# FFN of a two-layer streaming trunk: TensorE's steps written out, additions moved ahead of convolution taps; chunk scan with 128-column products, fewer TensorE instructions and a new order

## The reference

```python
def conv_ffn(h, buf, w_up, conv_w, conv_b, w_down):          # D_FF = 3072
    u, new_buf = causal_dwconv(h @ w_up, buf, conv_w, conv_b)  # 3 taps along time
    g, val = jnp.split(u, 2, axis=-1)
    return (jax.nn.gelu(g) * val) @ w_down, new_buf

def step(s, inp):                                             # RWKV-7, per head (16 heads of 64)
    r_t, w_t, k_t, v_t, aa_t, bb_t = inp
    sa = jnp.einsum('bhij,bhj->bhi', s, aa_t)
    s = s * w_t[:, :, None, :] + sa[..., None] * bb_t[:, :, None, :] + v_t[..., None] * k_t[:, :, None, :]
    return s, jnp.einsum('bhij,bhj->bhi', s, r_t)
...
for layer in range(DEPTH):
    hn = rmsnorm(x, norm_mix[layer])
    ...                                                       # y: RG-LRU mixer or RWKV-7 mixer
    x = x + y
    y, fb = conv_ffn(rmsnorm(x, norm_ffn[layer]), ...)
    x = x + y
```

## Time and profile before

| | us |
|---|---|
| median of 3 runs (lowest, highest) | 3423.7 (3421.11, 3430.75) |
| the profiled execution | 3425.41 |
| its span, first to last instruction | 3423.6 |
| PE busy | 3074.2 (90%) |
| DVE, ACT, POOL busy | 1705.8, 1156.4, 964.8 |

### The profile page before, as it was taken

How to read it: one execution, slowest core, us unless ns; L and a number is a source line. 1 busy time by engine, 2 the same in 40 slices (tenths; PEclk the granted TensorE clock), 3 DMA queues, 4 the chain that set the end, 5 groups by cost and what they waited for, 6 DMA issues and landing times.

```text
span 3423.6 us, 73739 instructions
## 1 busy us (share of the span) xinstructions
PE 3074.2 (90%) x32214; PEld 2966.1 (87%) x32214; DVE 1705.8 (50%) x1691; ACT 1156.4 (34%) x1334; POOL 964.8 (28%) x521
## 2 busy tenths in 40 slices
PE   5999699999999997699968888887899999999996
PEld 5888699999999997699957777776799999999996
DVE  6555654544454546102116776772464454444455
ACT  4634322211222214433326666664222221111222
POOL 2222232222222223213313334333222222222221
PEclk9999899999999998799979999998999999999998
DMA  2111011111111110332222122212111111111111
GB/s 97 42 41 39 25 38 44 44 43 43 43 43 43 43 44 19 137 128 83 89 88 61 52 66 67 67 33 88 38 38 44 38 44 44 44 38 38 44 44 64
DMA packets 87544, 185.80 MB, mean 54 GB/s; under 512 B 28896, under 2 KB 51936, under 8 KB 87264
## 3 DMA queue, kind: packets, MB, share of 16 engines
q1 hardware_dynamic: 80352, 154.73, 14.3%
q10 hardware_dynamic: 6912, 26.84, 1.9%
HBM read 145.01 MB, written 36.53 MB: 53 GB/s over the span
## 4 chain that ended last, share of the span: by engine, by line
PE 62%; issue 13%; DVE 12%; POOL 6%; ACT 5%; DMA 1%; SPq 0%; ACTq 0%; DVEq 0%; POOLq 0%
PE PS L1105 51%; PE PS L1270 10%; POOL WL L897 4%; DVE T L1545 3%; ACT T L461 2%; DVE T L1535 1%; POOL PL L897 1%; DVE X L1535 1%; DVE G L1535 1%; DVE HL L1535 1%; PE PS L1223 1%; POOL HL L897 1%; ACT L461 1%; DVE M L1550 1%; DVE NN L1535 1%
## 5 line engine op out<-in xcount | busy, mean ns | idle before, releaser
L897 POOL TENSOR_TENSOR WL<-RAW,WH 128x1024 fp32r<-128x1024 f32 x204 | 497.6, 2439 | 1586.3 <-ACT WH L461 1582.6
L1105 PE MATMUL PS<-HH,WH 128*128 128x364 f32 x3456 | 778.6, 334 | 91.1 <-POOL HL L897 42.8
L1105 PE MATMUL PS<-HH,WL 128*128 128x364 f32 x3456 | 774.4, 333 | 0.0
L1105 PE MATMUL PS<-HL,WH 128*128 128x364 f32 x3456 | 772.2, 332 | 0.0
L1105 PEld LDWEIGHTS PS<-HH,WH 128*128 128x128 f32 x3456 | 608.2, 191 | 104.0 <-issue 61.3
L1105 PEld LDWEIGHTS PS<-HH,WL 128*128 128x128 f32 x3456 | 612.6, 191 | 0.0
L1105 PEld LDWEIGHTS PS<-HL,WH 128*128 128x128 f32 x3456 | 610.4, 191 | 0.0
L1545 DVE SCALAR_TENSOR_TENSOR T<-T,FP 128x1092 f32<-128x1092 f32 x192 | 456.4, 2377 | 6.8
L1535 DVE TENSOR_TENSOR X<-PS,X 128x1092 f32<-128x1092 f32 x224 | 290.3, 1296 | 272.8 <-PE PS L1105 268.4
L461 ACT ACTIVATE WH<-RAW 128x1024 fp32r<-128x1024 f32 x204 | 216.6, 1062 | 408.8 <-PE PS L1105 388.3
L1550 DVE COPY T<-FP 128x2 f32<-128x2 f32 x96 | 16.3, 170 | 675.2 <-ACT T L461 675.2
(11 more groups left out here) (156 smaller groups left out, 3438.6 us busy)
## 6 DMA issues: line engine op xcount, KB each, us to landing
RAW<-weights SPq DMA_DIRECT2D x204, 512.0 KB, 3.4
scratch<-T ACTq DMA_DIRECT2D x32, 546.0 KB, 2.8
scratch<-SR ACTq DMA_DIRECT2D x16, 546.0 KB, 2.8
X<-xT SPq DMA_DIRECT2D x8, 546.0 KB, 7.7
yT<-T SPq DMA_DIRECT2D x8, 546.0 KB, 2.8
T<-scratch_m SPq DMA_DIRECT2D x8, 512.0 KB, 4.6
LW<-scratch SPq DMA_DIRECT2D x16, 192.0 KB, 2.7
KK<-scratch SPq DMA_DIRECT2D x16, 192.0 KB, 3.3
```

The costliest lines, as they stand in the source:

```text
L897: pool.tensor_tensor(out, full, hi, ALU.subtract).then_inc(*t.made(event))
L1105: mm = pe.matmul(acc[:, j, :], a, b[:, j * CW:(j + 1) * CW], start=(i == 0 and q == 0), stop=(i == len(blocks) - 1 and q == 2))
```

## The change

In the FFN, PE's loop over turns is gone and its steps are written out; the other engines keep their loops. DVE's `take(0)` goes ahead of tap 1, `take(1)` ahead of tap 0, and `take(2)` ahead of the product of gate and value. At the first FFN's end ACT's two `sh_hi` stand among the first four squares. In the scan, `solved` and the W half of `moves_and_left` make one 128-column product where there were two of 64 columns; `products` and `key_turn` load both halves of [b, k] of head 0 as 128 columns at once, three matmuls a chunk where there were four; SP waits for each of the five loads before it issues the next; and the order within the interval is new on PE, ACT, DVE and POOL.

```diff
 # SP, loads of job + 4
-                        sp.wait_ge(*t.at("k_g", 8 * (job + 2)))
+                        sp.wait_ge(*t.at("k_g", 6 * (job + 2)))
                         sp.wait_ge(*t.at("k_bonus", job + 2))
                     for tile, j in ((LW, 0), (KK, 4), (AA, 1), (RR, 3), (VV, 5)):
                         load(b, f, tile, j, f"dma_in{b}")
+                        if job >= -1:
+                            sp.wait_ge(*t.at(f"dma_in{b}", t.n[f"dma_in{b}"]))
...
 # ACT, norm behind the first FFN
-            for q in range(2):
-                act.wait_ge(*t.next("mu_w"))
-                run(TR[:, 6 + q, 0:D], T[:, q, 0:D], ACT.Copy, "sh_hi")
-            norm(m, added(m - KT), n, "two")
+            plus = added(m - KT)
+            def added_and_shift(k):
+                if k in (1, 3):
+                    act.wait_ge(*t.next("mu_w"))
+                    run(TR[:, 6 + k // 2, 0:D], T[:, k // 2, 0:D], ACT.Copy, "sh_hi")
+                plus(k)
+            norm(m, added_and_shift, n, "two")
...
 # PE, FFN
-                with pe.Fori(0, FFN_TURNS) as turn:
-                    t.enter(turn, FFN_TURN)
-                    a, b = m, n
-                    for s in (1, 2):
-                        a, b = step(a, b)
-                        a, b = down(a, b, s - 1)
-                    t.leave(FFN_TURNS)
-                m, n = m + 24 * FFN_TURNS, n + 12 * FFN_TURNS
+                for s in range(1, STEPS - 1):
+                    m, n = step(m, n)
+                    m, n = down(m, n, s - 1)
...
 # PE, scan
-                            mul(tile(3 + s, h, i - a), MT[HALF[1 - h], i, :], RA[HALF[1 - h], s, i - a, :],
-                                ("k_wv" if s else "k_w") if i == z - 1 else None)
+                            mul(PAIR[HALF[h], (i - a) * P:(i - a + 1) * P], MT[HALF[1 - h], i, :],
+                                RA[HALF[1 - h], i - a, :, :].rearrange("p s c -> p (s c)"), "k_w" if i == z - 1 else None)
...
+                            for h in range(HEADS):
+                                mul(PAIR[HALF[h], i * P:(i + 1) * P], W[HALF[h], i, :], G[HALF[h], a + i, h, CHUNK:],
+                                    "k_rp" if a + i == z - 1 else None)
...
+                        mul(PS[:, 3, (i - pa) * CHUNK:(i - pa + 1) * CHUNK], BK[HALF[0], i, :, :].rearrange("p s c -> p (s c)"),
+                            IST[HALF[0], :], end)
                         for s in range(2):
-                            for h in range(HEADS):
-                                mul(tile(3 + h, (h + s) % 2, i - pa), BK[HALF[h], i, s, :], IST[HALF[h], :],
-                                    "k_tb" if i == pz - 1 else None)
+                            mul(tile(4, 1 - s, i - pa), BK[HALF[1], i, s, :], IST[HALF[1], :], end)
...
 # DVE, conv: additions ahead of taps
                 for j in range(last - 1, -1, -1):
-                    if j == 0 and between is not None:
-                        take(between, 0)
                     back = last - j
+                    if between is not None:
+                        take(between + back - 1, back - 1)
...
 # DVE, order of an interval (first part)
                 near()
                 scan()
+                one_more()
                 key()
-                one_more()
+                grown(1)
                 centred()
                 weighted()
-                grown(1)
-                removal()
-                reading()
                 mask(2)
                 transfer()
+                reading()
                 grown(2)
+                removal()
```

More of the change, by code:

```diff
@@ L736, in bank, with pair @@
                     return PS[half, n, 0:chunks_ * CHUNK].rearrange("p (n c) -> p n c", c=CHUNK)
+                def pair(n, s, half=slice(0, P)):
+                    return PAIR[half, 0:n * P].rearrange("p (n s c) -> p n s c", s=2, c=CHUNK)[:, :, s, :]
                 def turned(k):
@@ L758, in spread_out @@
                         act.wait_ge(*t.next("k_ra", 4))
-                        run(RA[:, :, 0:z - a, :].rearrange("p s n c -> p s (n c)"), PS[:, 3:5, 0:(z - a) * CHUNK], ACT.Copy, "k_rae")
+                        run(RA[:, 0:z - a, :, :].rearrange("p n s c -> p s n c"),
+                            PS[:, 3:5, 0:(z - a) * CHUNK].rearrange("p s (n c) -> p s n c", c=CHUNK), ACT.Copy, "k_rae")
                 def norm_ln():
@@ L774, in solved_values @@
                     if has_s:
-                        act.wait_ge(*t.at("k_wv", 2 * job + 2))
+                        act.wait_ge(*t.at("k_w", 2 * job + 2))
                         for h in range(HEADS):
-                            run(UV[HALF[h], a:z, h, :], bank(4, z - a, HALF[h]), ACT.Copy, "k_sae")
+                            run(UV[HALF[h], a:z, h, :], pair(z - a, 1, HALF[h]), ACT.Copy, "k_sae")
                 def solved_keys():
@@ L782, in solved_keys @@
                         act.wait_ge(*t.at("k_w", 2 * job + 2))
-                        run(W[:, 0:z - a, :], bank(3, z - a), ACT.Copy, "k_we")
+                        run(W[:, 0:z - a, :], pair(z - a, 0), ACT.Copy, "k_we")
                 def decay_in():
@@ L1442, in products @@
                     for i in range(ga, gz):
+                        end = "k_g" if i == gz - 1 else None
+                        ar = [AR[HALF[h], i, :, :].rearrange("p s c -> p (s c)") for h in range(HEADS)]
+                        mul(PS[:, 3, (i - ga) * P:(i - ga + 1) * P], BK[HALF[0], i, :, :].rearrange("p s c -> p (s c)"), ar[0], end)
                         for s in range(2):
[L1444 to L1446 removed]
+                            mul(tile(4, 1 - s, i - ga, P), BK[HALF[1], i, s, :], ar[1], end)
                 def value_turn():
@@ L1483, in interval @@
                 means()
-                solved(0)
-                solved(1)
+                solved()
                 seed()
+                moves_and_left(2)
                 fresh_state()
-                moves_and_left(2)
+                grow(2)
+                variances()
                 fresh_out()
-                variances()
+                link(0)
+                left_times(3)
+                key_squares()
                 value_turn()
-                grow(2)
-                link(0)
-                key_squares()
-                left_times(3)
-                products(0)
                 link(1)
                 grow(3)
-                products(1)
+                link(2)
+                products(0)
+                link(3)
                 bonus_sums()
                 left_times(4)
-                link(2)
+                products(1)
+                grow(4)
                 key_turn()
-                link(3)
-                grow(4)
                 link(4)
-                lower(0)
                 left_times(5)
                 link(5)
+                lower(0)
                 lower(1)
@@ L1722, in step @@
                         if s and j:
-                            take(m + 1, 1)
+                            take(m + 2, 2)
                         dve.wait_ge(*t.next("gelu"))
@@ L1735, in ffn @@
                         a = step(s, a)
-                        take_all(a, False, first=2)
+                        take_all(a, False, first=3)
                         a += KT
@@ L1740, in ffn @@
                 m = step(STEPS - 1, m)
-                take_all(m, False, first=2)
+                take_all(m, False, first=3)
                 m += KT
@@ L1873, in masked @@
                         ga, gz = groups(pb, 4)[g]
[L1874 removed]
+                        dve.wait_ge(*t.next("k_g", 3))
                         n = gz - ga
@@ L1883, in transfer @@
                         dve.wait_ge(*t.at("k_rp", 2 * job + 2))
-                        tt(PT[:, 0:z - a, :], bank(4, z - a), wide(IST[:, :], z - a), ALU.add, "k_pp")
+                        tt(PT[:, 0:z - a, :], pair(z - a, 1), wide(IST[:, :], z - a), ALU.add, "k_pp")
                 def reading():
```

59 lines of the change are left out of this document (27 added, 32 removed).

## The result

The changed kernel takes 3517.5 us (median of 4 runs, 3504.8 to 3528.4), the kernel before beside it 3425.0 us (3421.1 to 3430.8): a ratio of 1.027, 95% interval 1.023 to 1.031. The prediction was 3333 us, range 3298 to 3368, faster with 0.95. It is slower by 92 us. The profiled execution took 3504.8 us, the fastest of the four, with a mean granted clock of 0.943 against 0.936 to 0.940 in the others.

The account below looks back on a forecast made before the run. PE was taken to bound the FFNs, and PE's work plus its waits the scan. Terms 33.2 + 25.6 + 7.4 + 9 + 5 + 10 = 90.2 us off 3425.4 gave 3335.2, predicted as 3333 us at the median, range 3298 to 3368.

Parts of the forecast that it names:

- Additions ahead of taps: Both FFNs: DVE's earlier additions end PE's 1.51 us wait in each of 22 steps; gain 33.2 us.
- ACT at the end of the first FFN: End of first FFN: squares start earlier, PE's 5.54 us wait and half the lower-clock time go; gain 7.4 us.
- PE's steps written out: Second FFN: four turn edges of PE's loop go, 6.39 us each; gain 25.6 us.
- Rivals 3: Second FFN: the turn-edge wait stays, as a delayed fetch met in straight code too; 3359 us, chance 0.05.
- 4: FFN steps: additions held up beside POOL, so the step's wait moves; 3345 us, chance 0.05.
- rival 5: Scan: SP's single loads come late and ACT waits for the keys, making the kernel slower; 3477 us, chance 0.03.
- Scan, 128-column products: Scan: gains in `solved` and `moves_and_left` outweigh losses in `products` and `key_turn`; gain 9 us, bounds +17 and -26.
- `products` then lose 0.10 us: Scan, six chunks and two recorded passes: a 128-column load makes `products` 115 ns a chunk and pass, from 107.
- `key_turn` ... +0.65 us: Scan, six chunks and two recorded passes: `key_turn` goes from 61 to 115 ns a chunk and pass.
- 53 ns for one stream of 128 columns in a row half: Scan: a 128-column stream fits under a pair's 59 ns load, so `solved` halves its pairs, -0.70 us for six chunks.
- fewer instructions: Scan: 816 matmuls fewer mean 13 instruction fetches fewer; gain 5 us, bounds 0 and 25.
- order and loads: Scan: half of the 13.1 us waits for B go, -6, and single loads no longer crowd DMA engines, -4; gain 10 us.

Follow-up runs that it names:

- experiment 3: Kernel before plus 13 patterns of float32 matmuls behind the second FFN, each timed alone; the mixed patterns took 0.78 (`products`) and 0.62 us (`key_turn`) a chunk.
- Experiment 6: Changed kernel with `products` and `key_turn` grouped by shape: all chunks' 128-column instructions first, then all 64-column ones; 3398.2 us, ratio 0.994.
- experiment 12: Kernel before plus seven further matmul patterns behind the second FFN, only the patterns timed; three that alternate shapes took rounds of 0.64, 0.54 and 0.64 us.
- experiment 4: Kernel before with only the FFNs' part: PE's steps written out, additions ahead of taps, ACT's two shift casts moved; 3360.6 us, ratio 0.981.
- 1: Also written experiment 1: changed kernel with `products` and `key_turn` as before, four 64-column instructions a chunk; 3337.9 us, ratio 0.976.
- experiment 8: Experiment 1 without the 128-column outputs: `solved` and `moves_and_left` with 64 moving columns, as before; 3361.5 us, ratio 0.983.
- 10: Experiment 1 without the wait on SP that lets the loads go one by one; 3338.3 us, ratio 0.976.
- Experiment 5: Changed kernel with `products` and `key_turn` as one 128-column instruction for each half, two a chunk in place of three; 3335.0 us, ratio 0.975.
- Experiment 2: Kernel before with only the changed kernel's new `products` and `key_turn`; 3545.9 us, ratio 1.037.

## Why the prediction was wrong

The FFNs' terms held. *Additions ahead of taps* and *ACT at the end of the first FFN* (16.6 + 7.4 = 24.0 us to the first norm): 23.5 in the profile. Second FFN (16.6 + 25.6 = 42.2): 43.6. *PE's steps written out* (25.6) gave 24.4 in its own stage. Rivals 3 and 4 did not come, nor did rival 5.

The steps that failed are in *Scan, 128-column products*.

- **"`products` then lose 0.10 us", "`key_turn` ... +0.65 us".** These terms were the cost of a wider load, with everything else overlapping as before. They measured 96 and 84 us in all, 4.2 and 3.7 us an interval. In parts, by an estimate from experiment 3: the wide stationary on one half has no partner beside it, 61 us; two changes of shape a chunk and function, 136 x (337 + 279 ns) = 84 us; the remaining 35 us I put down to the lower clock. Experiment 6 met the first part only with its own changes left out (22 us), so each part is good to some 20 us. The last is a remainder and not shown on its own: the clock fell behind such stretches in the scan and in the patterns (0.86 in the changed scan, 0.90 with `key_turn` alone new, 0.98 grouped). I had priced instructions by shape and never asked what two shapes next to each other do. The bound of +17 us was not a bound; the range should have had an end where nothing of the two functions overlaps. The trace of before had no mixture of widths on 64 rows, but it had changes of shape: not all scan matmuls lie on half of the rows, as I had written. In each interval two runs have stationaries of 128 rows and 64 columns, the first one here:

```profile
1976.51 0.92 PE L1270 MATMUL PS<-UV,G 128*64 128x64 f32 x24 [0.51 <-ACT UV L461]
1977.36 0.27 PE L1270 MATMUL PS<-G,W 64*64 64x64 f32 x2
```

Its last record starts at 1977.21 (1976.51 + 0.92 less 0.22), and the next shape 0.15 us later, where a step within the run is 0.03. So a price of this size for a change of shape could be read before the change was made; experiment 12 found it the same for rows as for columns.

- **"53 ns for one stream of 128 columns in a row half".** I had read 26.7 ns a record, two to a row half, as one stream of 53 ns. It is four quarters side by side, each with its own stream of 107 to 109 ns. So "128 columns fit under the same load" was wrong: a pair takes 109 ns with 128 columns and 59 with 64, and `solved` takes as long as before, as its rows show.
- The forecast for the whole scan was 24 us, with 17 us of loss in the two functions already taken off. The rest of the scan was to give 26 us by the 128-column outputs, 3 of the 5 by fewer instructions, and 10 by order and loads, 39 in all. It gave 22.6 us (from experiment 4 to 1), and by other steps: single loads nothing, order alone nothing, 128-column outputs alone nothing, order and outputs together 23 us. From experiment 8 to 1 PE's busy time in the scan fell by 11.5 us (442.9 to 431.4) and the instruction waits by 10.3 (64.0 to 53.7), which is most of the 23.5; why the outputs do this only in the new order is open. A sign of being wrong came as well: waits for ACT's `W` are 27.3 us in experiment 1, where those for `UV` were 9.0 before. They are 24.0 with the old `solved` too (experiment 8), so they belong to the new order. The waits for B, of which the new order was to take half away, stayed (12.1 us against 13.1).

Of the page that I had cited, TensorE: Matmul & The Clock Gate in the Trainium skill, the runs bear out the rule to 6 ns (112.6 ns from one matmul with a 128-column load to the next; 107 by the page). The rule that speaks of the loss is on another, which I had not weighed: the Trainium skill, TensorEngine Tiling (Array Packing), section Tiling Modes, says that a change of the tiling mode, unlike a change of tile, drains TensorE, and it lists 64x64 and 64x128 as two modes. The patterns agree and put a number on it, 0.14 to 0.17 us a change.

The best kernel here is that of experiment 1 (or 10), the change without its new `products` and `key_turn`: 3338 us, 2.4% below before. Experiment 5 is 3 us lower, but its scan computes other numbers.

## What to carry to other kernels

Before merging matmuls of part of the array into a wider one, list the shapes (rows by columns of the stationary) in program order and count the changes: here each cost 0.14 to 0.17 us, ten times a quarter's share of 15 ns, and more instructions of one shape beat fewer of two. If both shapes are needed, group them. And read a record's spacing together with how many array tiles are in flight: spacing times that number is the stream of one, which is what widening it doubles.

## What the runs showed of the hardware

- Work at 64 rows by 128 columns on both halves in turn takes 56 ns a record, and two such instructions replace four quarters in `products` at 224 ns for 216; the kernel with both functions built so lost nothing (experiment 5, 3335.0 us against 3337.9).
- The cost of a loop's edge is not fixed. Experiment 2 has the loop of the kernel before, and only 272 matmuls (544 records) fewer ahead of it, yet waited 4.8 us for instructions where the other waited 15.6. Its second FFN takes 914.7 us from norm to norm, 21.4 less than before. With code added only behind the loop the waits stayed (16.2 us in experiment 3, 15.5 in 12). So the place of the loop's code is a likely cause, but no run shows it by itself:

```profile
PEld PS L1105 <- DVE X L1537: 18.3, 11, 1.7
PEld PS L1105 <- issue: 4.8, 4, 1.4
```

So of the 24 us that straight code gave in the second FFN, some could have come by moving the loop; that was not tried.
- The clock fell in patterns in which PE was always busy by its records. It was 0.66 and 0.84 over the two mixed ones, 1.00 over four quarters, which last 1.6 us only (columns as in the earlier trace rows). It fell behind 128-column stationaries on the lower half alone too (L1571), so shape changes are not the only work that lets it fall: the 30 dense instructions behind these took 7.83 us instead of 5.27. It stayed at 1.00 over full ones of 128 rows, which last almost as long (L1582, 5.57 us), and the 30 dense ones behind those took 5.25.

```profile
3435.00:3443.70 8.70, 8.65 (x48) 5.19 (x48) 0.00 (x0) 0.00 (x0) 0.00 (x0) 0.66 0.01 2
3451.00:3456.70 5.70, 5.65 (x48) 4.41 (x48) 0.00 (x0) 0.00 (x0) 0.00 (x0) 0.84 0.00 0
3428.20:3429.80 1.60, 1.55 (x49) 1.38 (x49) 0.00 (x0) 0.00 (x0) 0.00 (x0) 1.00 0.00 0
```

```profile
3470.50 6.07 PE L1571 MATMUL PS<-RAW,RAW 64*128 64x64 f32 x48
3476.50 7.83 PE L1528 MATMUL PS<-HH,WH 128*128 128x364 f32 x30
```
